# Second half of v and the first stream's map back moved into the attention units, with one PSUM bank each for turned probabilities and values

## The reference

```
q, k, v = split(h @ w_qkv)            # q scaled by 64 ** -0.5
# context stream: keys are its own 128 tokens
p = softmax(q @ k.T);  o = p @ v
# latent stream: own 128 tokens (with bias and window mask) and 128 cached tokens
p = softmax(concat(q @ k.T + bias, q @ k_ctx.T));  o = p[:, :128] @ v + p[:, 128:] @ v_ctx
h = h + gate * (o @ w_o)
```

## Time and profile before

| | |
|---|---|
| median of 3 runs | 1832.34 us (1831.02 to 1832.8) |
| the profiled execution's own time | 1827.94 us |
| its span, first to last instruction | 1826.2 us |
| mean granted clock of TensorE | 0.976 |
| PE / DVE / ACT / POOL busy | 94% / 28% / 20% / 6% |
| chain that ended last | PE 76%, DMA 12%, DVE 6%, ACT 3% |

### The profile page before, as it was taken

One profiled execution on the slowest core, in us unless ns is written; L12 is line 12 of the kernel. 1 busy time (PEld: TensorE's weight loads), 2 busy tenths in 40 slices (PEclk: granted clock), 3 DMA queues, 4 the chain that ended last, 5 costly groups with the idle time before them and its releaser, 6 DMA issues.

```text
span 1826.2 us, 20719 instructions
## 1 busy us (share of the span) xinstructions
PE 1719.6 (94%) x8682; PEld 899.1 (49%) x8682; DVE 519.1 (28%) x1146; ACT 364.8 (20%) x703; POOL 104.8 (6%) x155
## 2 busy tenths in 40 slices
PE   5989999999998999989999999998999999899995
PEld 2444343367545444334864543435786654534441
DVE  1131221220442122230022212214334982312123
ACT  2031010121222111021201210103222661201111
POOL 1000000000000000000000000000001950000000
PEclk8999999999799999999999999999999999899998
DMA  9999999999349999998645999998864576599992
GB/s 388 355 420 427 426 427 427 401 350 345 116 163 407 426 428 426 427 367 333 222 184 196 400 428 426 427 425 329 305 242 158 136 245 235 209 429 425 427 427 116
DMA packets 92849, 614.07 MB, mean 336 GB/s; under 512 B 7505, under 2 KB 7729, under 8 KB 51409
## 3 DMA queue, kind: packets, MB, share of 16 engines
q1 hardware_dynamic: 85584, 585.36, 79.1%
q0 software_dynamic: 7168, 27.33, 4.7%
HBM read 608.34 MB, written 4.33 MB: 335 GB/s over the span
## 4 chain that ended last, share of the span: by engine, by line
PE 76%; DMA 12%; DVE 6%; ACT 3%; issue 3%; POOL 0%; SPq 0%; DVEq 0%; POOLq 0%; ACTq 0%
PE psum L1072 19%; PE psum L595 14%; PE psum L1107 12%; PE psum L588 12%; PE psum L1054 5%; DMA ring<-in_moe_w_down 5%; PE psum L1124 4%; PE psum L654 3%; DMA ring<-in_ada_w 3%; DMA arena<-in_moe_w_down 2%; DMA acc<-in_moe_w_down 1%; DVE arena L1796 1%; ACT arena L1407 1%; PE psum L1092 1%; PE psum L692 1%
## 5 line engine op out<-in xcount | busy, mean ns | idle before, releaser
L1072 PE MATMUL psum<-ring,arena 128*64 128x512 f32 x1152 | 342.9, 594 | 0.0
L588 PE MATMUL psum<-at,ring 128*128 128x256 f32 x1024 | 223.6, 380 | 0.0
L588 PEld LDWEIGHTS psum<-at,ring 128*128 128x128 f32 x1024 | 193.7, 190 | 28.4 <-issue 1.6
L1072 PE MATMUL psum<-arena 128*64 128x512 f32 x608 | 190.0, 594 | 0.0
L1107 PE MATMUL psum<-ring,arena 128*64 128x512 f32 x624 | 185.0, 599 | 5.0 <-DMA ring<-in_moe_w_down 2.9
L1072 PEld LDWEIGHTS psum<-ring,arena 128*64 128x64 f32 x1152 | 107.9, 137 | 165.3 <-issue 165.3
L1868 DVE TENSOR_TENSOR outtmp<-psum,gate 128x512 f32<-128x512 f32 x128 | 87.7, 685 | 333.9 <-PE psum L1124 333.9
L595 PE MATMUL psum<-ring,at 128*128 128x512 f32 (+1 forms) x416 | 172.5, 569 | 0.4 <-DVE at L1711 0.4
L1859 DVE TENSOR_TENSOR arena<-arena,psum 128x512 f32<-128x512 f32 x32 | 33.7, 1055 | 364.9 <-PE psum L1072 364.9
L1054 PE MATMUL psum<-arena,xn 128*128 128x128 f32 x1024 | 126.1, 284 | 6.4 <-issue 6.4
L1054 PEld LDWEIGHTS psum<-arena,xn 128*128 128x128 f32 x1024 | 122.7, 200 | 7.5 <-issue 7.5
(11 more groups left out here) (258 smaller groups left out, 1526.8 us busy)
## 6 DMA issues: line engine op xcount, KB each, us to landing
ring<-in_ada_w SPq DMA_DIRECT2D x43, 2048.0 KB, 11.1
ring<-in_moe_w_down SPq DMA_DIRECT2D x39, 2048.0 KB, 20.0
ring<-in_moe_w_up SPq DMA_DIRECT2D x38, 2048.0 KB, 15.2
ring<-in_moe_w_gate SPq DMA_DIRECT2D x34, 2048.0 KB, 17.7
arena<-in_moe_w_gate SPq DMA_DIRECT2D x22, 2048.0 KB, 13.4
arena<-in_moe_w_down SPq DMA_DIRECT2D x17, 2048.0 KB, 16.7
arena<-in_moe_w_up SPq DMA_DIRECT2D x16, 2048.0 KB, 18.5
ring<-in_ssd_w_in SPq DMA_DIRECT2D x12, 2048.0 KB, 9.5
```

What stands on the lines that cost most here:

```text
L588: last = nc.tensor.matmul(dst, slot(k)[:, c, m * P:(m + 1) * P], src[:, c, :], start=(c == 0), stop=(c == nk - 1))
L1072: last = nc.tensor.matmul(ps[b][e * CAP:(e + 1) * CAP, :], rows, slot_half(k + e, 4, h)[:, c, :], start=(h == 0 and c == 0), stop=(h == 1 ...
```

## The change

The loop over Q0 to Q5 ends with Q4. The eight matmuls of each stream for Q5 (`second_values`) and the sixteen of the first stream's map back (`first_stream_map`) are called one by one from a `filler` inside the unit loop, at three places of each step. The turned probabilities use bank 4 alone, the weighted values bank 6 alone; banks 5 and 7 take the fillers' results. DVE copies the second half of v in its turns 3 and 5 and does the first stream's two adds in turns 16 and 18. ACT gets a wait behind its loop.

```diff
-            return (((4, 5), (2, 3)), ((4, 5), (6, 3)), ...
+            return (((4, 5), (2, 3)), ((5, 4), (7, 3)), ...
...
-                    for j in range(6):
+                    for j in range(5):
...
+                    pe.wait_ge(qk_ev, 8)
...
-                    pe.wait_ge(v_ev, 4)
+                    pe.wait_ge(v_ev, 2)
+
+                    def second_values(x):
+                        k = AT[n, "Q5"]
+                        s, c = divmod(x, DC)
+                        if x == 0:
+                            arrive(k)
+                        last = nc.tensor.matmul(ps[5 + 2 * s][:, :], at[:, c, s * P:(s + 1) * P], slot(k)[:, c, :],
+                                                start=(c == 0), stop=(c == DC - 1))
+                        if c == DC - 1:
+                            last.then_inc(slot_done if s else v_mm, 1)
+
+                    def first_stream_map(x):
+                        j, c = divmod(x, DC)
+                        k = AT[n, f"O{j}"]
+                        if x == 0:
+                            pe.wait_ge(ot_ready, DC)
+                            pe.wait_ge(v_ev, 4)
+                        if c == 0:
+                            arrive(k)
+                        last = nc.tensor.matmul(ps[out_bank(n, j, 0)][:, :], oT[:, c, 0:P], slot(k)[:, c, :],
+                                                start=(c == 0), stop=(c == DC - 1))
+                        if c == DC - 1:
+                            last.then_inc(o_mm, 1)
+
+                    def filler(i, part):
+                        x = 3 * i + part
+                        if x < 2 * DC:
+                            second_values(x)
+                        x = 3 * (i - 12) + part
+                        if 0 <= x < 2 * DC:
+                            first_stream_map(x)
...
                     def prob_transposes(u):
-                        if u >= 2:
-                            pe.wait_ge(pt_ready, u - 1)
+                        if u >= 1:
+                            pe.wait_ge(pt_ready, u)
                         for b in range(2 * (1 + s)):
-                            last = nc.tensor.transpose(bank(4 + u % 2, 4, P)[:, b, :],
+                            last = nc.tensor.transpose(bank(4, 4, P)[:, b, :],
...
                     def weighted_values(u):
-                        if u >= 2:
-                            pe.wait_ge(ot_ready, u - 1)
+                        if u >= 1:
+                            pe.wait_ge(ot_ready, u)
+                        if u == 4:
+                            pe.wait_ge(v_ev, 4)
...
-                            dst = ps[6 + u % 2][HD * hh:HD * (hh + 1), 0:P]
+                            dst = ps[6][HD * hh:HD * (hh + 1), 0:P]
...
                     for i in range(U + 3):
                         if i < U:
                             scores(i)
+                        filler(i, 0)
                         if 2 <= i <= U + 1:
                             prob_transposes(i - 2)
+                        filler(i, 1)
                         if i >= 3:
                             weighted_values(i - 3)
+                        filler(i, 2)
                     pe.wait_ge(ot_ready, U)
-                    map_part(n, 0, 0, 0, oT, 1)
-                    map_part(n, 0, 1, 0, oT, 1)
                     map_part(n, 1, 0, 0, oT, 1)
...
# ACT, behind its loop over the units
+                    act.wait_ge(av_mm, U)
...
# DVE, in its turn i, behind the copy to oT
+                        if i in (3, 5):
+                            s = (i - 3) // 2
+                            if s:
+                                dve.wait_ge(slot_done, AT[n, "Q5"] + 1)
+                            else:
+                                dve.wait_ge(v_mm, 2)
+                            V.tensor_copy(vtok[:, s, 512:1024], ps[5 + 2 * s][:, :]).then_inc(v_ev, 1)
+                        if i in (16, 18):
+                            mixer_add(n, (i - 16) // 2, [AT[n, "O0"], AT[n, "O1"]])
                     dve.wait_ge(kv_out, 32)
-                    add_mixer(n, [AT[n, "O0"], AT[n, "O1"]])
+                    add_mixer(n, [AT[n, "O0"], AT[n, "O1"]], 2)
```

More of the change, by code:

```diff
@@ L362, in out_bank @@
         def out_bank(n, j, s):
-            return (((4, 5), (2, 3)), ((4, 5), (6, 3)), ((4, 5), (6, 3)), ((5, 6), (7, 3)))[n][j][s]
+            return (((4, 5), (2, 3)), ((5, 4), (7, 3)), ((4, 5), (6, 3)), ((5, 6), (7, 3)))[n][j][s]
         def row_bank(x, i):
@@ L790, in _ @@
                             for s in range(S):
-                                b = 2 * (j - 4) + s
-                                pe.wait_ge(qk_ev, 5 + b)
-                                last = dense_tok(k, s, ps[b][:, :])
+                                pe.wait_ge(qk_ev, 5 + s)
+                                last = dense_tok(k, s, ps[s][:, :])
                                 last.then_inc(slot_done if s else v_mm, 1)
@@ L1308, in _ @@
                             w = 2 * P * (1 + v // DC)
-                            A(probT[:, v % 2, 0:w], ps[4 + v % 2][:, 0:w], ACT.Copy).then_inc(pt_ready, 1)
+                            A(probT[:, v % 2, 0:w], ps[4][:, 0:w], ACT.Copy).then_inc(pt_ready, 1)
+                    act.wait_ge(av_mm, U)
                 elif l == 2:
@@ L1558, in modulation, with mixer_add, add_mixer @@
                                            g.unsqueeze(2).to_broadcast([P, DC, S]), ALU.add, ALU.mult).then_inc(gsc_ready, 1)
-            def add_mixer(n, k_last):
+            def mixer_add(n, i, k_last):
+                s, j = divmod(i, 2) if n else (i % 2, i // 2)
+                if s:
+                    dve.wait_ge(slot_done, k_last[j] + 1)
+                else:
+                    dve.wait_ge(o_mm, 2 * n + j + 1)
+                if i == 0:
+                    dve.wait_ge(gate_in, 16 * (2 * n + 1))
+                cols = slice(j * 512, (j + 1) * 512)
+                if n == 3:
+                    dve.wait_ge(yrstd, s + 1)
+                    link(V.scalar_tensor_tensor(outtmp[:, i % 2, :], ps[out_bank(n, j, s)][:, :], stat[:, 16 + s:17 + s], gate[:, 0, s, cols],
+                                                ALU.mult, ALU.mult))
+                else:
+                    link(V.tensor_tensor(outtmp[:, i % 2, :], ps[out_bank(n, j, s)][:, :], gate[:, 0, s, cols], ALU.mult))
+                V.tensor_tensor(hid[:, s, cols], hid[:, s, cols], outtmp[:, i % 2, :], ALU.add).then_inc(h_ready, 1)
+            def add_mixer(n, k_last, added=0):
                 t = 2 * n + 1
@@ L1564, in add_mixer @@
                     s, j = divmod(i, 2) if n else (i % 2, i // 2)
[L1565 to L1578, removed]
+                    if i >= added:
+                        mixer_add(n, i, k_last)
                     if n and i == 2:
@@ L1680, in _ @@
                     modulation(n, 2)
[L1681 to L1687, removed]
+                    for s in range(S):
+                        if s:
+                            dve.wait_ge(slot_done, AT[n, "Q4"] + 1)
+                        else:
+                            dve.wait_ge(v_mm, 1)
+                        V.tensor_copy(vtok[:, s, 0:512], ps[s][:, :]).then_inc(v_ev, 1)
                     for h in range(2):
@@ L1710, in _ @@
                             dve.wait_ge(av_mm, v + 1)
-                            V.tensor_copy(oT[:, j, s * P:(s + 1) * P], ps[6 + v % 2][:, 0:P]).then_inc(ot_ready, 1)
+                            V.tensor_copy(oT[:, j, s * P:(s + 1) * P], ps[6][:, 0:P]).then_inc(ot_ready, 1)
+                        if i in (3, 5):
+                            s = (i - 3) // 2
+                            if s:
+                                dve.wait_ge(slot_done, AT[n, "Q5"] + 1)
+                            else:
+                                dve.wait_ge(v_mm, 2)
+                            V.tensor_copy(vtok[:, s, 512:1024], ps[5 + 2 * s][:, :]).then_inc(v_ev, 1)
+                        if i in (16, 18):
+                            mixer_add(n, (i - 16) // 2, [AT[n, "O0"], AT[n, "O1"]])
                     dve.wait_ge(kv_out, 32)
-                    add_mixer(n, [AT[n, "O0"], AT[n, "O1"]])
+                    add_mixer(n, [AT[n, "O0"], AT[n, "O1"]], 2)
                 elif l == 2:
```

## The result

The changed kernel takes 1836.09 us (median of 8 runs, 1833.83 to 1837.91) against 1831.68 us (8 runs, 1828.41 to 1833.16) for the kernel before on the same chip: ratio 1.0029, interval 1.0019 to 1.0038. That is 5.3 us slower (3.5 to 7.0). Its profiled span is 1832.1 us, before 1826.2. The profiled execution, 1833.83 us, is the fastest of the eight.

A forecast was written before the change was run, and what follows sets the result against it. Units bound first by PE at half clock, then by DVE at full clock. Logits 2.7 us earlier, plus 3.9 us for the clock, net +1.2 on the median 1832.34: 1833.5 us, range 1825 to 1840.

The forecast's parts named there:

- The loop: Attention units: with one values bank, each step pays scores, DVE's whole turn, 0.05 us signalling, then values, in sequence.
- steps 9 to 11: Unit steps of stream 1 without dense fill, at full clock: 3.29, 3.29 and 3.57 us.
- bank waits don't bind: Rival, chance 0.10: steps without fill keep DVE's old pace, 6.9 us less, no clock fall; net -9.6, 1822.7 us.
- The turned probabilities' bank at nothing: Attention units: the single bank's wait for ACT's copy costs nothing; if late, at most 0.6 us in four steps.
- The clock: PE drops to half clock among the attention units' steps without fill, for some 8 to 12 us, costing 3.9 us.
- bare steps: Unit steps without dense fillers between the two filled groups; PE idle for over half of 3.05 to 3.29 us.
- The first rival: Chance 0.30: the clock stays up through the units, all else as forecast without the 3.9 us: 1829.6 us.
- the filled steps: Unit steps with three dense matmuls each, 0 to 4 and 12 to 16; full clock expected, signs of about 4.4 us.
- Steps 0 to 4: First unit steps, scores plus three Q5 matmuls each: 2.95, 2.95, 3.27, 3.58, 3.58, together 16.3 us.
- steps 12 to 14: Unit steps of stream 1 with three matmuls of the first stream's map each: 4.44 us each.
- step 15 and the tail: End of the units: step 15 at 4.44 us, step 16 at 3.78, step 17 and the end with it 7.9 together.
- Edits costed at nothing: Later loads, later v and k outputs, the first stream's norm and ACT's new wait: no cost expected.

The follow-up runs named there:

- useless_dense: The changed kernel plus eight dense matmuls with unused results, two in each of steps 8 to 11: 3.5 us slower than the kernel before.
- two_v_banks: The changed kernel with a second bank for the weighted values of units 3, 5, 7 and 9: 5.1 us faster than the kernel before.
- two_t_banks: The changed kernel with a second bank for the turned probabilities of units 5 and 7: ratio 1.0046 to the kernel before.
- changed_again: The changed kernel unaltered, run once more: 5.1 us slower than the kernel before.
- grouped_fill: The changed kernel with each step's three fillers together behind the scores: steps 3 and 4 from 3.98 to 3.79 us, 13 and 14 from 4.74 to 4.45.

## Why the prediction was right and where it was off

- *The loop.* Right, in place and nearly in size. The forecast's full-clock loop for steps 9 to 11 was 3.29, 3.29 and 3.57; `useless_dense` shows 3.46, 3.45 and 3.67. Most of the difference is the signal from DVE's copy to the values, priced at 0.05 us and 0.15 in step 9 (495.52 to 495.67), and the values of stream 0, priced at 0.31 and 0.37 in step 8 (492.21 to 492.58). The rival "bank waits don't bind" fell: it priced the loop at 6.9 us, and `two_v_banks`, less the 3.1 us of the clock, shows 6.5 gone when a second bank is there. The Trainium skill ("TensorE: Matmul & The Clock Gate", "HAM oscillation — how this bites in real kernels") reports a kernel in which a second PSUM buffer gained nothing more; this does not carry over to this loop, where a second bank takes 9.6 us out of the stretch.
- *The turned probabilities' bank at nothing.* Right in the changed kernel (`two_t_banks`), with the limit that it becomes the next wait once the values have two.
- *The clock.* It fell in the bare steps, at 494.0, in step 9 as forecast, and came back in step 12. Its price was 3.1 us against 3.9 forecast; in `changed_again`, which fell in step 7, it was 4.6 (100.2 less the 95.6 of `useless_dense`), so step 9 and the 3.1 us fit one profile of the kernel and not the other. It was low for 13.7 us, and 8 to 12 were forecast. The first rival (clock stays up) is out. The Trainium skill ("TensorE: Matmul & The Clock Gate", "Why this matters for your kernels") warns of long idle gaps between bursts of matmuls. Short gaps did not keep the clock here: in the changed kernel it fell inside a gap of 1.99 us, with none over 1.8 before it, and in `changed_again` inside one of 0.94, with none over 1.2 before it.
- *The mis-sized terms: the filled steps, and the bare ones a little.* The sum of the units at full clock was 61.3 us; `useless_dense`, which has no fall, takes 64.75 (466.24 to 530.99), 3.4 more. Steps 0 to 4 took 17.8 and not 16.3, steps 12 to 14 14.2 and not 13.3, steps 5 to 11 1.0 more in all; step 15 and the tail were as worked out. So 2.4 us of the 3.4 are the filled steps. A filler was priced at its rate in a dense run: three fillers before scores take 2.78 us and not 2.61 (465.46 to 468.24), and standing apart they take more, as `grouped_fill` shows. The scores before them take 0.42 and not 0.35 (465.04 to 465.46), a price that was half of one at half clock. With 3.4 more and 0.8 less for the clock the forecast shift of +1.2 becomes +3.8, and +4.1 was measured in the profile. For the same reason the logits start at 547.7, outside the 540 to 546 that were named as a sign.
- *The outcome.* The time lay in the range, which is 15 us wide, and the sign was the forecast's, which is partly luck: +1.2 us is less than the 3.7 that the prediction says a measurement can tell. "Within 0.2%" held 0.63 of the chance and the loss is 0.29%; without the 3.4 us above it would have been within.
- *Edits costed at nothing* (loads, outputs, the norm beside the map): nothing of them shows up to the logits. The dense part behind the units took 14.8 us as worked out, and no DMA wait stands between the units and the logits, nor in the 90 us behind them. The longer low clock behind the logits was not among the terms.

## What to carry to other kernels

When two engines pass work through one PSUM bank, look at where in its turn the reader empties it: a reader that does so last, behind work that waits for the writer's newest result, closes a loop, and its whole turn is paid in every step. Independent dense work was free here only inside that wait, so spread it over the steps that wait and put none where the engine is already full. In these profiles it also kept the clock up, so that even useless dense products shortened the stretch.

## What the runs showed of the hardware

The place of the clock's fall varies from run to run of one program: in step 9 in one profile of the changed kernel, in step 7 in another, with 13.7 and 20.5 us at half clock and 1.5 us of difference in the stretch. Eight added matmuls, priced at 0.87 us each, in steps where PE idled half the time, kept TensorE at 2.4 GHz in the units, and the stretch was 3.1 us shorter. A dense float32 matmul of 512 columns takes 0.87 us from start to start in a dense run, 0.96 between scores and a turning (475.27 to 476.23), and 1.06 before scores (477.77 to 478.83).
